# Differential attention: three pairs of score banks, scores a slot ahead, maps combined before normalizing

## What is computed

```python
def diff_attention(h, w_qkv, q_gain, k_gain, ..., sub_gain, lam_init, cos, sin):
    q, k, v = jnp.split(h @ w_qkv, 3, axis=-1)          # H = 8 heads, D = 64, two maps c per head
    q = apply_rope(rms_norm_2(q, q_gain), cos, sin).reshape(B, S, H, 2, D)
    k = apply_rope(rms_norm_2(k, k_gain), cos, sin).reshape(B, S, H, 2, D)
    v = v.reshape(B, S, H, 2 * D)
    for i in range(S // BLOCK):                         # BLOCK = 128
        n_k = (i + 1) * BLOCK
        s = einsum('bqhcd,bkhcd->bhcqk', q_blk, k[:, :n_k]) * scale
        p = softmax(where(kpos <= qpos, s, -inf), axis=-1)
        a = p[:, :, 0] - lam * p[:, :, 1]
        outs.append(einsum('bhqk,bkhe->bqhe', a, v[:, :n_k]))
    o = rms_norm_2(concatenate(outs, axis=1), sub_gain) * (1.0 - lam_init)
```

## Time and profile before

| | us |
|---|---|
| median of 3 runs | 3277.34 (3276.47 to 3284.27) |
| profiled execution | 3274.17 |
| its span | 3272.4 |
| PE busy | 2959.1 (90%) |
| PEld busy | 2408.5 (74%) |
| DVE busy | 1744.0 (53%) |
| ACT busy | 1169.0 (36%) |
| POOL busy | 1137.7 (35%) |
| the stage `diff`, from the barrier at 1527.1 to the next product at 1655.8 | 128.7 |

### The profile page before, as it was taken

How to read it: one execution, slowest core, us unless ns; L and a number is a source line. 1 busy time by engine, 2 the same in 40 slices (tenths; PEclk the granted TensorE clock), 3 DMA queues, 4 the chain that set the end, 5 groups by cost and what they waited for, 6 DMA issues and landing times.

```text
span 3272.4 us, 40478 instructions
## 1 busy us (share of the span) xinstructions
PE 2959.1 (90%) x13820; PEld 2408.5 (74%) x13820; DVE 1744.0 (53%) x2211; ACT 1169.0 (36%) x1874; POOL 1137.7 (35%) x502
## 2 busy tenths in 40 slices
PE   5989999998779999898789999889898798899999
PEld 4767778877667888686457888668786697778887
DVE  7565848455876373674852222666467636542112
ACT  2473523224334322333632333333343433332222
POOL 3312444433014444443134444434204340044443
PEclk9999999989899999999999999889998899989999
DMA  5243445532002333232013333223102230023332
GB/s 187 85 154 125 161 133 173 176 95 72 7 29 85 93 96 96 78 92 59 7 51 90 97 96 92 77 66 91 40 1 69 69 90 7 18 78 91 96 96 90
DMA packets 364853, 278.79 MB, mean 85 GB/s; under 512 B 13362, under 2 KB 320947, under 8 KB 363699
## 3 DMA queue, kind: packets, MB, share of 16 engines
q1 hardware_dynamic: 363472, 276.76, 27.9%
q10 hardware_dynamic: 1251, 0.33, 0.0%
HBM read 274.96 MB, written 2.10 MB: 85 GB/s over the span
## 4 chain that ended last, share of the span: by engine, by line
PE 61%; DVE 9%; ACT 3%; issue 2%; POOL 0%; DVEq 0%; ACTq 0%; POOLq 0%
PE banks L883 12%; PE banks L878 11%; PE banks L887 11%; PE banks L848 5%; PE banks L851 5%; PE banks L845 5%; DVE tmp L1934 2%; PE banks L1115 1%; PE banks L816 1%; DVE Z L2117 1%; DVE small L2072 1%; PE banks L1183 1%; DVE h_lo L480 1%; PE banks L1059 0%; PE banks L1083 0%
## 5 line engine op out<-in xcount | busy, mean ns | idle before, releaser
L722 POOL TENSOR_TENSOR w_lo<-w_raw,w_hi 128x1024 fp32r<-128x1024 f32 (+1 forms) x424 | 1037.5, 2447 | 1763.2 <-ACT w_hi L1294 1761.8
L1294 ACT ACTIVATE w_hi<-w_raw 128x1024 fp32r<-128x1024 f32 (+1 forms) x424 | 445.4, 1051 | 1233.1 <-PE banks L887 792.1
L848 PE MATMUL banks<-w_hi,h_lo 128*128 128x512 f32 x960 | 384.3, 400 | 34.4 <-DVE h_lo L480 26.3
L845 PE MATMUL banks<-w_hi,h_hi 128*128 128x512 f32 x960 | 390.8, 407 | 22.6 <-ACT h_hi L1429 19.3
L851 PE MATMUL banks<-w_lo,h_hi 128*128 128x512 f32 x960 | 382.9, 399 | 0.7 <-POOL w_lo L722 0.7
L878 PE MATMUL banks<-h_hi,w_hi 128*128 128x512 f32 x1280 | 345.5, 398 | 18.6 <-ACT h_hi L1427 9.8
L883 PE MATMUL banks<-h_lo,w_hi 128*128 128x512 f32 x1280 | 322.4, 392 | 5.7 <-DVE h_lo L480 3.8
L878 PEld LDWEIGHTS banks<-h_hi,w_hi 128*128 128x128 f32 x1280 | 245.1, 192 | 80.7 <-issue 21.6
L883 PEld LDWEIGHTS banks<-h_lo,w_hi 128*128 128x128 f32 x1280 | 240.9, 188 | 62.2 <-DVE h_lo L478 6.6
L887 PE MATMUL banks<-h_hi,w_lo 128*128 128x512 f32 x1152 | 284.5, 389 | 0.0
L848 PEld LDWEIGHTS banks<-w_hi,h_lo 128*128 128x128 f32 x960 | 200.3, 209 | 72.9 <-DVE h_lo L480 29.9
(11 more groups left out here) (284 smaller groups left out, 4626.9 us busy)
## 6 DMA issues: line engine op xcount, KB each, us to landing
w_raw<-in_m_w_up SPq DMA_DIRECT2D x64, 512.0 KB, 3.9
w_raw<-in_m_w_down SPq DMA_DIRECT2D x64, 512.0 KB, 4.0
Z<-in_ada_w SPq DMA_DIRECT2D x48, 512.0 KB, 4.8
w_raw<-in_kv_w SPq DMA_DIRECT2D x48, 512.0 KB, 3.6
w_raw<-in_ffn_w_gate SPq DMA_DIRECT2D x44, 512.0 KB, 3.8
w_raw<-in_ffn_w_up SPq DMA_DIRECT2D x44, 512.0 KB, 3.9
tmp<-in_ada_w SPq DMA_DIRECT2D x32, 512.0 KB, 4.7
w_raw<-in_ffn_w_down SPq DMA_DIRECT2D x32, 512.0 KB, 4.0
```

The lines of the kernel that those rows point to most:

```text
L722: pool.tensor_tensor(wlo[j][:, 0:n], raw[j][:, 0:n], whi[j][:, 0:n], ALU.subtract).then_inc(s_wlo, 1)
L845: pe.matmul(t, hh, wh, start=k == 0, stop=False)
L848: pe.matmul(t, hl, wh, start=False, stop=False)
L1294: act.activation(whi[par][:, 0:kc * P], raw[par][:, 0:kc * P], ACT.Copy).then_inc(s_whi, 1)
```

## The change

- Scores use three pairs of banks (0 to 5). A score product waits for the exponentials of slot s-3 instead of s-2, and PE's list has scores(s+1) at the head of slot s, with scores(0) ahead of the loop.
- The transposes use bank 6 alone, and the mean square uses it too; the value products move to bank 7. turn_map(s) waits until map s-1 is taken and until the logarithm has read the last mean square. mean_square(h) is now behind turn_map in the slot's list, and waits until the map that was turned just before it is taken.
- The maps are combined without normalizing: first + second * ratio, with ratio = -lambda * l1 / l2 (l1, l2 the row sums), so the result is l1 times the old one. One scaling of a whole map becomes one product of a single column. The RMS norm that follows removes the factor, if EPS is scaled by l1 squared: DVE makes P * EPS * l1 * l1 for the four slots of a head at once (`scale_eps`), and PE adds it in the mean square, by four more 128-column fp32 products with the identity. The logarithm no longer adds eps.
- ACT's `scale` moves from the end of a head's last slot to the front of the next slot 0; `square`, `take_map`, `probs` keep their order. On DVE `sub_norm` moves from slot 0 to slot 1, `sub_low` from slot 2 to slot 3.
- Opening: ACT copies head 0's high parts (POOL did), DVE clears the halves of the k tiles for head 0, POOL clears those for head 1, and PE waits for POOL's clearing only at head 1.

```diff
         def diff_scores(s, c):
-            return bank[2 * (s % 2) + c]
+            return bank[2 * (s % 3) + c]
...
+        def diff_sums(s, n=1):
+            return sums8[:, 8 + 2 * (s % 8):8 + 2 * (s % 8) + 2 * n]
...
@@ POOL
-                for h in range(8):
+                for h in range(1, 8):
+                    pool.wait_ge(e["high_parts"], past(3 * h))
                     pool.wait_ge(e["scores"], past(NB * (h - 1)))
...
+                if kind == "diff":
+                    todo = [qk[64:128, 5 * S:6 * S], qk[64:128, 7 * S:8 * S], qk[0:64, 9 * S:10 * S], qk[0:64, 11 * S:12 * S]]
@@ PE
-                zero_rows_in(2)
...
                     pe.wait_ge(e["low_parts"], past(3 * h + 3))
-                    pe.wait_ge(e["probs"], past(2 * s - 2))
+                    if s == NB:
+                        zero_rows_in(4)
+                    pe.wait_ge(e["probs"], past(2 * s - 4))
...
                     pe.wait_ge(e["combined"], past(s + 1))
-                    pe.wait_ge(e["taken"], past(s - 1))
+                    pe.wait_ge(e["taken"], past(s))
+                    pe.wait_ge(e["log_mean"], past((s + BEHIND - NB) // NB))
...
                     pe.wait_ge(e["squares"], past(h + 1))
-                    pe.wait_ge(e["log_mean"], past(h))
-                    pe.matmul(bank[7], ones, zt(28), start=True, stop=True).then_inc(e["mean_square"], 1)
-
+                    pe.wait_ge(e["taken"], past(min(NB * h + 2 * NB - BEHIND, DIFF_SLOTS)))
+                    pe.wait_ge(e["eps_scaled"], past(h + 1))
+                    pe.matmul(bank[6], ones, zt(28), start=True, stop=False, skip_group_check=True)
+                    for s in range(NB * h, NB * h + NB):
+                        _, b = diff_slot(s)
+                        mm = pe.matmul(bank[6][:, b * P:(b + 1) * P], diff_eps(s).to_broadcast([P, P]), ident, start=False, stop=s == NB * h + NB - 1, skip_group_check=True)
+                    mm.then_inc(e["mean_square"], 1)
+
+                scores(0)
                 for s in range(DIFF_SLOTS + BEHIND):
-                    if s < DIFF_SLOTS:
-                        scores(s)
+                    if s + 1 < DIFF_SLOTS:
+                        scores(s + 1)
                     h, i = divmod(s, NB)
-                    if i == NB - 1 and h:
-                        mean_square(h - 1)
                     if s >= BEHIND:
                         turn_map(s - BEHIND)
+                        if i == NB - 1 and h:
+                            mean_square(h - 1)
                         if i == (BEHIND - 1) % NB and h:
                             values(h - 1)
@@ ACT
+                act.activation(q_hi[0], zt(0), ACT.Copy).then_inc(e["high_parts"], 1)
+                for r, t in zip(HALF, k_hi):
+                    act.activation(t[0][r, :], zrows(r, 8), ACT.Copy).then_inc(e["high_parts"], 1)
...
                     if i == NB - 1 and h:
                         square(h - 1)
+                    if i == 0 and h >= 2:
+                        scale(h - 2)
                     if s >= BEHIND:
                         take_map(s - BEHIND)
                     if s < DIFF_SLOTS:
                         probs(s)
-                    if i == NB - 1 and h:
-                        scale(h - 1)
-                    if i == 1 and h >= 2:
+                    if i == 2 and h >= 2:
                         y_high(h - 2)
@@ DVE
+                def first_parts():
+                    for par in range(2):
+                        rows = qk[HALF[1 - par], (4 + 4 * par) * S:(8 + 4 * par) * S].rearrange("p (t n) -> p t n", n=2 * S)[:, :, 0:S]
+                        dve.memset(rows.bitcast(F32), 0.0)
+                    low_q(0)
...
-                    dve.wait_ge(e["combined"], past(s - 3))
-                    dve.reciprocal(inv, diff_small(s, 1)).then_inc(e["inverted"], 1)
+                    dve.wait_ge(e["combined"], past(s - 1))
+                    dve.reciprocal(inv, l2).then_inc(e["inverted"], 1)
                     dve.wait_ge(e["inverted"], past(s + 1))
-                    dve.tensor_scalar(second, second, inv[:, 1:2], lamv, ALU.mult, ALU.mult).then_inc(e["second_scaled"], 1)
-                    dve.wait_ge(e["second_scaled"], past(s + 1))
-                    dve.scalar_tensor_tensor(first, first, inv[:, 0:1], second, ALU.mult, ALU.subtract).then_inc(e["combined"], 1)
+                    dve.scalar_tensor_tensor(ratio, inv, minus_lam, l1, ALU.mult, ALU.mult).then_inc(e["ratio"], 1)
+                    dve.wait_ge(e["ratio"], past(s + 1))
+                    dve.scalar_tensor_tensor(first, second, ratio, first, ALU.mult, ALU.add).then_inc(e["combined"], 1)
+
+                def scale_eps(h):
+                    l1 = diff_sums(NB * h, NB).rearrange("p (s c) -> p c s", c=2)[:, 0, :]
+                    dve.wait_ge(e["probs"], past(2 * NB * h + 2 * NB))
+                    dve.wait_ge(e["mean_square"], past(h - 1))
+                    dve.scalar_tensor_tensor(diff_eps(NB * h, NB), l1, P * EPS, l1, ALU.mult, ALU.mult).then_inc(e["eps_scaled"], 1)
...
                     if s:
                         combine(s - 1)
-                    if i == 0 and h >= 2:
+                    if i == 0 and h:
+                        scale_eps(h - 1)
+                    if i == 1 and h >= 2:
                         sub_norm(h - 2)
                     if i == 1 and h < 7:
                         low_q(h + 1)
                     if i >= 2 and h < 7:
                         low_k(h + 1, i - 2)
-                    if i == 2 and h >= 2:
+                    if i == 3 and h >= 2:
                         sub_low(h - 2)
+                sub_norm(6)
                 sub_low(6)
```

More of the change, by code:

```diff
@@ L384, in program @@
                         ("high_parts", "low_parts", "values_in", "block_scores", "reduced", "neg_max", "diagonal", "scores", "probs", "values_added", "inverted", "output", "output_high", "output_low", "max_spread", "sink_or_denominator", "squares_or_taken")}
-        df = {e: sem(f"diff_{e}") for e in ("high_parts", "low_parts", "scores", "neg_max", "probs", "inverted", "second_scaled", "combined", "turned", "taken", "values_added", "squares", "mean_square", "log_mean", "rms_scale", "normed", "output_high", "output_low")}
+        df = {e: sem(f"diff_{e}") for e in ("high_parts", "low_parts", "scores", "neg_max", "probs", "inverted", "ratio", "eps_scaled", "combined", "turned", "taken", "values_added", "squares", "mean_square", "log_mean", "rms_scale", "normed", "output_high", "output_low")}
         stk = {e: sem(f"stick_{e}") for e in ("high_parts", "low_parts", "values_in", "scores", "abs", "exp", "log", "softplus", "suffix_sums", "weights", "values_added", "output_high", "output_low")}
@@ L615, in diff_scores, with diff_neg_max, diff_ratio, diff_eps @@
         def diff_scores(s, c):
-            return bank[2 * (s % 2) + c]
+            return bank[2 * (s % 3) + c]
         def diff_probs(s, c):
             return tmp[2 * (s % 4) + c]
-        def diff_small(s, what):
-            return sums8[:, 8 * what + 2 * (s % 4):8 * what + 2 * (s % 4) + 2]
+        def diff_neg_max(s):
+            return sums8[:, 2 * (s % 4):2 * (s % 4) + 2]
+        def diff_sums(s, n=1):
+            return sums8[:, 8 + 2 * (s % 8):8 + 2 * (s % 8) + 2 * n]
+        def diff_ratio(s):
+            return sums8[:, 24 + 2 * (s % 2):25 + 2 * (s % 2)], sums8[:, 25 + 2 * (s % 2):26 + 2 * (s % 2)]
+        def diff_eps(s, n=1):
+            return sums8[:, 28 + s % 8:28 + s % 8 + n]
         block = ctx.enter_context(nc.Block())
@@ L742, in _ @@
                 if kind in ("stick", "attn", "diff"):
-                    zero_rows(n_bars, kind == "attn" and st["mode"] == "dil")
+                    zero_rows(n_bars, st["mode"] if kind == "attn" else kind)
                 if kind == "diff":
@@ L1172, in turn_map @@
                     pe.wait_ge(e["combined"], past(s + 1))
-                    pe.wait_ge(e["taken"], past(s - 1))
+                    pe.wait_ge(e["taken"], past(s))
+                    pe.wait_ge(e["log_mean"], past((s + BEHIND - NB) // NB))
                     for kb in range(b + 1):
-                        mm = pe.transpose(bank[4 + s % 2][:, kb * P:(kb + 1) * P], diff_probs(s, 0)[:, kb * P:(kb + 1) * P], ident)
+                        mm = pe.transpose(bank[6][:, kb * P:(kb + 1) * P], diff_probs(s, 0)[:, kb * P:(kb + 1) * P], ident)
                     mm.then_inc(e["turned"], 1)
@@ L1182, in values @@
                     for kb in range(NB):
-                        mm = pe.matmul(bank[6][:, kb * P:S], zt(16 + h)[:, kb * P:(kb + 1) * P], zt(24 + kb)[:, kb * P:S],
+                        mm = pe.matmul(bank[7][:, kb * P:S], zt(16 + h)[:, kb * P:(kb + 1) * P], zt(24 + kb)[:, kb * P:S],
                                        start=kb == 0, stop=kb == NB - 1, skip_group_check=True)
@@ L1618, in take_map @@
                     act.activation(zt(24, b + 1).rearrange("p (k q) -> p k q", q=S)[:, :, b * P:(b + 1) * P],
```

(14 more changed lines are left out.)

25 lines of the change are left out of this document (13 added, 12 removed).

## The result

The changed kernel takes 3296.7 us (median; 3294.2 to 3297.5) where the kernel before takes 3276.9 beside it (3273.8 to 3284.3): a ratio of 1.0056, 95% interval 1.0038 to 1.0074, so 19.8 us slower. The profiled execution of after took 3296.43 us, span 3294.6. The forecast was 3290.9 with 3280 to 3302: sign and range hold, but the sum was too small. Where the sum had +13.5, the stage alone shows +26.0.

The account below looks back on a forecast made before the run. TensorE bounds the kernel, DVE paces this stage; the change closes a ring through PE. Terms -2.8 - 0.75 - 1.3 + 10.0 + 4.0 + 4.4 = +13.5 us on 3277.34 gave 3290.9, range 3280 to 3302.

Parts of the forecast that it names:

- The ring: Differential attention: turning map 0 and mean square behind scores awaiting low_k1; 15.6 us a head for 13.66, five heads +10.0.
- low_k1: DVE's differential attention step for the second half of k, the last operand a head's first scores wait for; cuts the heads.
- scores 1: The next head's second score products on PE, queued behind mean square and eps; 1.39 us.
- opening: Start of the differential attention, up to its first scores: about 1532.2 instead of 1534.96, -2.8 us (-2.4 to -3.8).
- head 1's part: Head 1, with no mean square before it yet: 13.4 us for 14.72, -1.3 (-2 to -0.5).
- Rival 1: Faster: DVE stays the bound, as if turning never waited for low_k1; 11.9 us a head, -13.4, 3264 us; 13%.
- rival 2: Same: The ring holds, but the clock stays up and values are low; sum +3 to +9, 3284 us; 23%.
- Rival 3: More: slow clock takes 1.7 in each ring and again at other pauses; +20 to +30, 3302 us; 9%.
- Clock: Half clock on scores and mean square after PE's 2.9 us pause: 0.8 us a head (0 to 1.7), +4.0 for five.
- End: Stage end, last maps one at a time through one bank: +2.7, eps +0.9, clock +0.8; +4.4 us (3 to 6).
- T: The end of low_k1 for the coming head, taken as time zero; head 7's value products forecast at 19.3 us.
- Head 0: First head of the differential attention, where DVE alone sets the pace in three slots: -0.75 us.

Follow-up runs that it names:

- clock_kept: The changed kernel with nine 512-column bf16 products put into PE's pause ahead of its wait for low_k1; 3292.0 us, beside 3283.0 of the kernel before.
- both_moved_kept: The changed kernel, map 0 turned before scores, both low k parts in slot 2, weight split held back, two bf16 products before value products; 3261.3 us, ratio 0.9951.
- low_k_early_before: The kernel before with both low halves of k made in slot 2 on DVE; 3269.9 us, beside 3278.7 of the kernel before.
- combine_alone: The kernel before with only the new combining and eps products, keeping its banks, PE order and opening; 3282.5 us, beside 3278.7 of the kernel before.
- both_moved: The changed kernel with map 0 turned ahead of the next head's first scores and both low halves of k in slot 2; 3267.2 us, ratio 0.9966.

## Why the prediction was right, and where its sizes failed

**Right in kind, step by step.** The bound was read rightly: the order on PE decides, not DVE's busy time. The ring's terms against after and clock_kept, whose clock is 1.00: mean square released 3.10 after low_k1, measured 3.14 (1573.36 to 1576.50); mean square and eps 1.8, measured 1.74; scores 1 1.39, measured 1.38; exponentials 1.48, measured 1.48; reciprocal and ratio 0.4, measured 0.45; DVE from the combining of slot 0 to low_k1 6.5, measured 6.3 (1602.65 to 1608.98); whole ring 15.6, measured 15.41. Five of them are 77.1 us for 67.8, +9.2 where +10.0 stood. DVE's work a head -0.9, measured -0.95; opening -2.8, measured -2.7; head 1's part -1.3, measured -1.2. Rival 1 is excluded by the rows of the ring, rival 2 by PEclk 0.77 to 0.90 in all five heads. Rival 3 is not excluded: in the stage, the slow clock in every ring and at other places too is what came, and the stage's +26.0 lies in its +20 to +30, which had 9%.

**Clock: the step that was too small.** I took 0.8 a head, a middle between none and 1.7, for want of a row that decided. Against the 15.41 of clock_kept it was 1.6 in each of the three heads in the middle, 2.9 in the first (18.28) and 3.3 in the last (18.74): 11.0 where 4.0 stood. In the middle heads the same pause of 2.4 us repeats ahead of the same scores. In the first and the last the half clock lies on the mean square and eps as well, which was in no term. In the last head they are, behind a pause of 4.57 us that the collision had made longer:

```profile
1628.19 0.80 PE L1179 MATMUL banks<-qk_parts 128*128 128x512 f32 x1 [4.57 <-DVE qk_parts L2207]
...
1633.18 2.05 PE L1209 MATMUL banks<-Z,ones_r 128*128 128x512 f32 x2 [0.73 <-issue]
1635.02 1.78 PE L1212 MATMUL banks<-squares,head_sums 128*128 128x128 f32 x8
```

In the first head the pause was only 1.90 us; why the half clock began later there and reached the mean square, no run tells. Five heads: 9.2 + 11.0 + 2.16 = 22.4, which closes the sum.

**Collision: not in the sum at all.** 2.16 us in one head. In before the same weight split lay at 1616.07, 2.56 us long, beside DVE's pause. A step on another queue that was hidden by a pause had to be walked past when the pause moved; I did it for POOL's casts, not for its next stage's work.

**End.** Head 7's value products start 21.4 us after T, forecast 19.3. PE at the end of the stage in after, against the earlier trace rows:

```profile
1662.65 1.10 PE L1209 MATMUL banks<-Z,ones_r 128*128 128x512 f32 x2 [0.79 <-ACT Z L1649]
...
1666.56 0.41 PE L1192 MATMUL banks<-squares,tmp 128*128 128x128 f32 x2 [0.63 <-issue]
1667.48 0.45 PE L1192 MATMUL banks<-squares,tmp 128*128 128x128 f32 x1 [0.52 <-issue]
1668.30 4.63 PE L1200 MATMUL banks<-Z 128*128 128x512 f32 x8 [0.37 <-ACT Z L1642]
1673.62 2.07 PE L1209 MATMUL banks<-Z,ones_r 128*128 128x512 f32 x2 [0.69 <-ACT Z L1649]
1675.48 1.92 PE L1212 MATMUL banks<-squares,head_sums 128*128 128x128 f32 x8
```

The three maps do go one at a time through one bank, with pauses of 0.63 and 0.52 between. The mean square of head 6 starts at 15.8, where it was to end: the 1.6 of the first scores and a little more. The value products take 4.63 for 4.12, and the last mean square with eps about 3.8 us at half clock where 1.8 was reckoned. So 4.8 + 0.5 + 2.55 = 7.85 for 4.4; by these rows the excess is clock but for some tenths. No run shows the end of after with the clock up; with map 0 turned first and a granted clock of 0.98 (both_moved_kept) it is 27.4 us.

**Head 0** gained 0.35, not 0.75. The rows of DVE in both kernels add it up: of the three scalings that were replaced, two saved 0.1 and 0.2 us and the third nothing, since its product of one column took 0.60 us beside GpSimd's cast (1541.22 to 1541.82); DVE also waited 0.27 us for scores; and a low part that had taken 1.09 us took 0.68.

**Luck.** The kernel's +19.8 is inside the range because things outside the stage were kind: the rest of the kernel gave -3.7 in the profiled execution, and the profile of before, to which the stage is compared, was itself 2.7 us under the median beside after. By the stage's +26.0 on the 3277.34 shown, the time would have been 3303, just outside.

## What to carry to other kernels

Before an instruction is put ahead of another on an in-order queue, ask what the first one waits for and whether the second was what that very thing needed: here a step of 1.3 us moved past a wait closed a ring of 15.4. Work saved on the busiest engine is worth only what the next wait leaves (0.66 us a head saved, 0.08 gained), and a pause in which another queue's transfer or subtraction was hidden is part of the schedule. A cost with two levels can come in every repeat (five heads of five in after, three of five in low_k_early_before, one of five in combine_alone), so the range has to reach as far as all of them, and to every product that stands behind the pause.

## What the runs showed of the hardware

- The length of one pause doesn't tell whether the clock falls. Ahead of the value products a pause of 0.76 us is followed by products at full clock in after (2.39 us, 1659.03) and at half clock in both_moved (4.08 us, 1590.47); one of 1.44 in low_k_early_before by 2.42 us in one head and 4.00 and 4.06 in the next two; one of 1.50 in combine_alone by 4.11 and then 2.42. What went before in the head differs. Nor does it take one long pause: in the steady heads of after none is above 2.42 us, and the clock falls in each.
- Cheap products in a pause keep the clock up: nine bf16 products in the 2.4 us pause gave 1.6 us a head back, two in one of 0.75 gave 0.6. They can also only shift the half clock: in clock_kept the value products of head 6 took 3.91 us where they took 2.39 in after.
- DVE against GpSimd, each with two operands in SBUF: 2.83 us for 0.69, longer by about what was left of the other's instruction (2.28 us). Against a cast, which reads one operand, and even for a single column: the [128 x 1] product takes 0.22 us, but 0.45 in slot 1 of the steady heads of after (1588.38, 1605.37, 1622.38), and 2.00 at most (both_moved_kept). In the twelve traces with the new combining, 41 of 384 of these products take longer than 0.26 us, and each ends within 0.02 us of the end of a GpSimd instruction. The bounds were 0.15 to 0.30.
